# The first block product behind three norms on unscaled input, with the norm's factor applied to its result

## The reference

```python
def rms_norm(x, g):
    xf = x.astype(jnp.float32)
    y = xf * lax.rsqrt(jnp.mean(xf * xf, axis=-1, keepdims=True) + RMS_EPS)
    return (y * g.astype(jnp.float32)).astype(x.dtype)

def modulate(xn, shift, scale):
    return xn * (1.0 + scale) + shift

def sq_relu_mlp(u, w1, w2):
    a = jnp.maximum(u @ w1, 0.0)
    return (a * a) @ w2
...
    h = h + g1 * y
    h = h + g2 * sq_relu_mlp(modulate(rms_norm(h, norm2_g[l]), sh2, sc2), w_mlp1[l], w_mlp2[l])
```

## Time and profile before

| | |
|---|---|
| median of 3 runs | 2055.06 us |
| lowest and highest | 2051.90, 2056.86 us |
| the profiled execution | 2056.09 us |
| its span (first to last instruction) | 2054.2 us |
| mean granted clock of TensorE | 0.987 of full |
| PE busy | 97% |
| POOL, DVE, ACT busy | 45%, 45%, 32% |

### The profile page before, as it was taken

How to read it: one execution, slowest core, us unless ns; L and a number is a source line. 1 busy time by engine, 2 the same in 40 slices (tenths; PEclk the granted TensorE clock), 3 DMA queues, 4 the chain that set the end, 5 groups by cost and what they waited for, 6 DMA issues and landing times. The chain is left out here.

```text
span 2054.2 us, 25743 instructions
## 1 busy us (share of the span) xinstructions
PE 2002.2 (97%) x10096; PEld 1633.8 (80%) x10096; DVE 930.8 (45%) x1422; ACT 667.1 (32%) x872; POOL 920.0 (45%) x704
## 2 busy tenths in 40 slices
PE   7998899999999999999999999999999999999998
PEld 3886578888888888888888866888888878888887
DVE  0546885755748352323233265266664433223123
ACT  2322553222212332212223355356554232222122
POOL 2333345545555535445445312543444455444445
PEclk9899999999999989999999999999999999999999
DMA  8144341625334222222222202222222222222221
GB/s 350 57 143 150 131 152 75 246 91 194 147 153 175 84 83 92 102 102 83 101 102 89 82 22 78 82 83 83 72 73 82 103 82 89 96 102 100 85 82 42
DMA packets 42629, 222.92 MB, mean 109 GB/s; under 512 B 12721, under 2 KB 13233, under 8 KB 17329
## 3 DMA queue, kind: packets, MB, share of 16 engines
q1 hardware_dynamic: 42544, 221.77, 30.0%
HBM read 217.55 MB, written 2.10 MB: 107 GB/s over the span
## 5 line engine op out<-in xcount | busy, mean ns | idle before, releaser
L880 POOL TENSOR_TENSOR wl<-raw,wh 128x512 fp32r<-128x512 f32 x611 | 836.4, 1400 | 1010.9 <-ACT wh L495 911.7
L982 PE MATMUL bank<-uh,wh 128*128 128x512 f32 x1480 | 590.8, 399 | 2.2 <-DVE ul L1472 0.5
L984 PE MATMUL bank<-uh,wl 128*128 128x512 f32 x1480 | 576.9, 390 | 0.0
L983 PE MATMUL bank<-ul,wh 128*128 128x512 f32 x1480 | 576.7, 390 | 0.0
L495 ACT ACTIVATE wh<-raw 128x2048 fp32r<-128x2048 f32 (+1 forms) x149 | 281.3, 1888 | 589.6 <-PE bank L984 586.8
L982 PEld LDWEIGHTS bank<-uh,wh 128*128 128x128 f32 x1480 | 277.8, 188 | 76.8 <-issue 11.1
L984 PEld LDWEIGHTS bank<-uh,wl 128*128 128x128 f32 x1480 | 277.8, 188 | 59.2
L983 PEld LDWEIGHTS bank<-ul,wh 128*128 128x128 f32 x1480 | 278.0, 188 | 58.1 <-issue 3.6
L982 PE MATMUL bank<-ah,wh 128*128 128x512 f32 x816 | 321.3, 394 | 0.0
L984 PE MATMUL bank<-ah,wl 128*128 128x512 f32 x816 | 320.3, 393 | 0.0
L983 PE MATMUL bank<-al,wh 128*128 128x512 f32 x816 | 317.5, 389 | 0.0
(11 more groups left out here) (228 smaller groups left out, 1982.5 us busy)
## 6 DMA issues: line engine op xcount, KB each, us to landing
raw<-in_w SPq DMA_DIRECT2D x64, 1024.0 KB, 5.5
mraw<-in_w_modr SPq DMA_DIRECT2D x32, 1024.0 KB, 4.9
raw<-in_w_gu SPq DMA_DIRECT2D x22, 1024.0 KB, 4.9
raw<-in_w_hg SPq DMA_DIRECT2D x16, 1024.0 KB, 5.0
modf<-in_w_modf SPq DMA_DIRECT2D x8, 1024.0 KB, 17.9
raw<-in_w_in SPq DMA_DIRECT2D x8, 1024.0 KB, 16.7
raw<-in_w_out SPq DMA_DIRECT2D x8, 1024.0 KB, 6.0
mmid<-in_w_modr SPq DMA_DIRECT2D x8, 1024.0 KB, 4.9
```

The lines of the kernel that those rows point to most:

```text
L880: last = pool.tensor_tensor(wl[:, b % 2, k:k + 2], raw[:, b % RAW, k:k + 2], f32(wh[:, b % 2, k:k + 2]), ALU.subtract)
L982: pe.matmul(out, ah_, bh, start=first, stop=False)
L983: pe.matmul(out, ah_, bl, start=False, stop=False)
L984: return pe.matmul(out, al_, bh, start=False, stop=last)
```

## The change

At three norms, `mlp0` (block 12), `mix2` (block 80) and `ffn` (block 121), block one no longer reads the normed input. It reads high and low parts of h times the norm's gain only, `ah`/`al` (`mh`/`ml` at `mix2`). ACT writes the high part right behind each chunk's square (`plain_highs`), DVE the low part behind the addition to h (`plain_lows`). PE does the sums of the norm behind k = 1 of that block and the spread behind k = 3 (`first_product`), with no `keep_clock` there. Since the norm's factor belongs to a token, that is to a column of the result, DVE multiplies block one's result by it afterwards (`first_scale`): it copies the spread factor from its bank to `rsb` within `norm`, and behind `norm` writes bank times `rsb` into the two `tt` buffers. ACT then reads `tt` where it read the bank.

At `mlp0` the input has a shift too. Its product with block one's weights is made as a column: 16 matmuls of `raw` against the shift on PE ahead of block 11 (`shift_columns`), copied to `ccol` by DVE, and used as the bias of ACT's ReLU. Block two and all later ones read the normed input as before.

ACT splits block two no longer within `highs` but whole, between the square and plain high of chunk 6 and those of chunk 7. The set of `mod_columns` and `mod_store` that stood behind block two, four and six of mlp0's first group stands one block later. The loops of which block one was part are written out in part (mlp0's first group, mlp1's last on DVE) or in full (the FFN). The gain of `mlp0` is made before the output projection, and SP waits for block 80 and not 79 before it loads `wmask`, since `mh` and `ml` lie where it goes.

The core of the diff:

```diff
+        def plain(name):
+
+            return (mh, ml) if name == "mix2" else (ah, al)
+
+        def plain_gain(name, k):
+
+            if name == "mlp0":
+                return gm[:, 2, k:k + 1]
+            c = (V_MIX if name == "mix2" else V_FFN) + k
+            return vec[:, c:c + 1]
...
+                    if j == 4:
+                        sp.wait_ge(ccol_full, 1)
...
-                if j == 2:
-                    wait_block(sp, b0 - 1)
+                if j == 3:
+                    wait_block(sp, b0)
...
+            def plain_highs(name, ks):
+
+                for k in ks:
+                    h_wait(act, name, k)
+                    if name == "mlp0" and k == 0:
+                        act.wait_ge(gain_ready, 3)
+                    act.activation(plain(name)[0][:, k, :], h[:, k, :], ACT.Identity, scale=plain_gain(name, k)).then_inc(xhi_ready, 1)
+
+            def statistics(name, ks):
+
+                for k in ks:
+                    squares(name, h, (k,))
+                    if name in EARLY:
+                        plain_highs(name, (k,))
...
-            squares("mlp0", h, (6, 7))
+                    statistics("mlp0", (2 * (b - 9), 2 * (b - 9) + 1))
+            statistics("mlp0", (6,))
+            split(FIRST["mlp0"] + 1)
+            statistics("mlp0", (7,))
...
+                            if first and j == 0:
+                                act.wait_ge(bank_free[bi], used(b0) + 1)
+                                act.wait_ge(ccol_ready, 1)
+                                act.wait_ge(square_ready, SQ0 + 32 * layer + m - 1)
+                                act.activation(r1[:, m % 2], tt[:, half], ACT.Relu, bias=ccol[:, half:half + 1]).then_inc(first_done, 1)
+                                continue
...
+                            if j < 7 or after not in EARLY:
+                                statistics(after, (2 * (j - 4), 2 * (j - 4) + 1))
+                            else:
+                                statistics(after, (6,))
+                                split(b0 + 33)
+                                statistics(after, (7,))
...
-            highs("mlp0", lambda k: mod(0, 3, k), uh, beside=FIRST["mlp0"] + 1)
+            highs("mlp0", lambda k: mod(0, 3, k), uh)
...
+                    out, col = (aqT[:, 2 * j + half, :], V_BQ + 2 * j + half) if j < 4 else (akT[:], V_BK)
+                    if j == 0:
+                        act.wait_ge(bank_free[bi], used(b0) + 1)
+                        act.activation(out, tt[:, half], ACT.Identity, bias=vec[:, col:col + 1]).then_inc(first_done, 1)
+                        continue
...
+                    scaled = not per and n == 0
+                    act.wait_ge((bank_free if scaled else bank_full)[bi], used(b, q, per) + 1)
...
+                    act.activation(gs[:, half], tt[:, half] if scaled else bank[bi][:], ACT.Sigmoid).then_inc(gs_ready, 1)
...
+            def norm_spread(name, n=S):
+
+                i, rms = NORM[name], norm_banks(name)[1]
                 pe.wait_ge(rstd_ready, i + 1)
                 for a in range(n // P):
                     last = pe.matmul(rms[:, P * a:P * a + P], rc[:, 1, a:a + 1].to_broadcast([P, P]), ident, start=True, stop=True)
                 last.then_inc(rms_full, 1)
+
...
+            def first_product(name, b):
+
+                def ready(k):
+                    if k == 2:
+                        norm_sum(name)
+                    if k == 4:
+                        norm_spread(name)
+                    pe.wait_ge(xlo_ready, 8 * EARLY[name] + k + 1)
+
+                product(b, *plain(name), ready=ready)
 
...
+            def shift_columns(b):
+                pe.wait_ge(raw_full[b % RAW], 16 * (b // RAW + 1))
+                for half in range(2):
+                    for k in range(KC):
+                        last = pe.matmul(bank[4][:, half:half + 1], raw[:, b % RAW, k, P * half:P * half + P], mod(0, 3, k), start=(k == 0), stop=(k == KC - 1))
+                last.then_inc(ccol_full, 1)
+
             for b in range(8, 12):
+                if b == 11:
+                    shift_columns(FIRST["mlp0"])
...
+                        if first and j == 0:
+                            first_product("mlp0", b0)
+                        elif j < 4:
+                            product(b0 + j, uh, ul, q, 8, ready=normed(f"mlp{layer}") if j == (1 if first else 0) else None)
                         else:
...
+                    if k == 0 and name in EARLY:
+                        dve.tensor_copy(rsb[:], rms[:]).then_inc(rsb_ready, 1)
...
+            def plain_lows(name, ks):
+
+                hi, lo = plain(name)
+                for k in ks:
+                    dve.wait_ge(xhi_ready, 8 * EARLY[name] + k + 1)
+                    dve.scalar_tensor_tensor(lo[:, k, :], h[:, k, :], plain_gain(name, k), f32(hi[:, k, :]), ALU.mult, ALU.subtract).then_inc(xlo_ready, 1)
+
+            def first_scale(name, b):
+
+                for half in range(2):
+                    bi = bank_of(b, half)
+                    dve.wait_ge(bank_full[bi], used(b) + 1)
+                    if half == 0:
+                        dve.wait_ge(rsb_ready, EARLY[name] + 1)
+                        dve.wait_ge(ulo_ready, 8 * NORM[name] + 8)
+                    dve.tensor_tensor(tt[:, half], bank[bi][:], rsb[:], ALU.mult).then_inc(bank_free[bi], 1)
 
...
+                    dve.wait_ge(ccol_full, 1)
+                    dve.tensor_copy(ccol[:], bank[4][:, 0:2]).then_inc(ccol_ready, 1)
```

More of the change, by code:

```diff
@@ L52 @@
           "ffn": FIRST["wout2"], "final": FIRST["ffn"] + 30}
+EARLY = {"mlp0": 0, "mix2": 1, "ffn": 2}
 MOD0 = 16
@@ L673, in _ @@
             mlp(1, "mix2")
-            highs("mix2", None, uh, beside=FIRST["aq"] + 1)
+            highs("mix2", None, uh)
             act.wait_ge(lb_ready, 1)
@@ L1258, in _ @@
                 last.then_inc(yp_full, 1)
-            norm_sum("mlp1")
+            normalise("mlp1")
             mlp(1)
-            norm_sum("mix2")
             b0 = FIRST["aq"]
-            for j in range(4):
-                product(b0 + j, uh, ul, ready=normed("mix2") if j == 0 else None)
+            first_product("mix2", b0)
+            for j in range(1, 4):
+                product(b0 + j, uh, ul, ready=normed("mix2") if j == 1 else None)
             def half_and_half(b, first_by_token, q=0, per=0):
@@ L1623, in _, with group @@
                     mod_store(MOD_MID // 2 + (b - 8) // 2)
+            plain_lows("mlp0", (6, 7))
             dve.wait_ge(mcol_used, MOD0 // 2)
-            gain_of(2, modc[:, 32:40], vec[:, V_G2:V_G2 + 8])
             def mlp(layer):
                 b0, n0 = FIRST[f"mlp{layer}"], 32 * layer
-                with dve.Fori(0, 4) as q:
+                def group(q, last=False, first=False):
                     for j in range(8):
+                        if first and j == 0:
+                            first_scale("mlp0", b0)
                         if layer == 0 and j < 6:
@@ L1636, in mlp @@
                                 add_to_h(b0 + j, m, mod(layer, 5, m), q, 8)
+                                if last and j > 4:
+                                    plain_lows("mix2", (m - 2,))
                                 continue
@@ L1639, in mlp @@
                             dve.wait_ge(bank_free[bi], used(b0 + j, q, 8) + 1)
+                            if first and j == 0:
+                                dve.wait_ge(first_done, 2 * EARLY["mlp0"] + half + 1)
                             dve.wait_ge(a_lo, SQ0 + n0 + m - 1 + 8 * q)
@@ L1906, in _ @@
             dve.memset(stat[:, 4, 1:2], 0.0).then_inc(zv_ready, SQ0)
-            with dve.Fori(0, 2) as q:
+            first_scale("ffn", b0)
+            for q in range(2):
                 for j in range(0, 8, 2):
-                    hidden(j, j, j, q, 12)
+                    hidden(12 * q + j, 8 * q + j, j)
                 for j in range(8, 12):
                     for half in range(2):
-                        add_to_h(b0 + j, 2 * (j - 8) + half, None, q, 12)
+                        add_to_h(b0 + 12 * q + j, 2 * (j - 8) + half, None)
             for j in range(0, 6, 2):
```

110 lines of the change are left out of this document (69 added, 41 removed).

## The result

The changed kernel takes 2066.64 us (median of 5 runs, 2064.91 to 2070.26), the kernel before 2055.06 in the same session (5 runs, 2051.90 to 2056.86): a ratio of 1.0061, 95% interval 1.0050 to 1.0072. It is slower, by 11.6 us; 2067.0 was forecast. In a second session the changed kernel took 2067.86 beside 2055.71. The profiled execution of after was the slowest of its five (2070.26, span 2068.4), so the traces lie 14.2 us apart and the medians 11.6.

What follows compares the result with a forecast made beforehand. PE, busy 97% of the span, was taken as the bound. Later third blocks 1.6, shift's product 3.9 and clock loss 6.6 made 12.1 us, so about 2067 against 2055.06; range 2058 to 2073.

Steps and rivals of the forecast that it cites:

- Block one starts at T, PE is through with block two at T+25.2: At each norm, T being when PE ends the block before: PE runs blocks one and two without waiting until T+25.2.
- DVE's norm starts at T+8.7: At each norm, DVE's norm starts once the spread has landed, 8.7 us after PE ends the block before; previously T+4.8.
- The third block at T+31.6, 31.2 and 30.2: Block three's start at mlp0, mix2 and ffn, set by its weights, counted from PE's end of the block before.
- in all 1.6 us: Block three's lateness against before, like for like: 0.8 at mlp0, 0.5 at mix2, 0.3 at ffn.
- Stalls of 6.4, 6.0 and 5.0: PE stands still between blocks two and three at mlp0, mix2 and ffn for these times in us.
- The shift's product, 3.9: Ahead of block 11, 32 one-column records take 3.9 us of PE's time; bounds 3.6 and 7.3.
- Rival 3: Narrow products also lower the clock: 1.9 us more on the shift's product, 1.7 for what follows; 2070.8 us, chance 0.12.
- The clock behind the stalls, 6.6: Half clock after each of PE's three stalls costs 2.2 us, the mean of two earlier stalls; ends 0 and 8.3.
- Rival 1: The same chain at the three norms, but the clock holds: 2060.6 us, chance 0.18.
- The sum: Whole kernel: late third blocks, shift's product and clock loss add 12.1 us, giving about 2067 us.
- Rival 2: Block three's weights are ready at T+25.2 at each norm: 15.8 us gained, less 3.9; 2043 us, chance 0.10.

Runs made afterwards that it cites:

- experiment 8: The changed kernel with the product that spreads the sums issued one pair of passes earlier in block one, at all three norms: 2063.10 us, ratio 1.0037.
- experiment 3: The changed kernel with 20 keep-clock products on PE ahead of block three at each of the three norms: 2061.36 us, ratio 1.0037.
- experiment 7: The changed kernel with the early block at mix2 and ffn only, block three's weights split early there, no shift product: 2042.85 us, ratio 0.9944.
- experiment 6: The changed kernel with block three's weights split early, block four's transfer ahead of the modulation loads, shift product in one piece: 2048.93 us, ratio 0.9970.
- experiment 10: experiment 7 with the shift's product added ahead of block eleven, its result read by nothing: 2049.73 us, ratio 0.9970.
- experiment 9: experiment 7 without its early split: block three's weights split where the changed kernel splits them: 2059.20 us, ratio 1.0020.

## Why the prediction was right, step by step

**Block one starts at T, PE is through with block two at T+25.2.** Shown: block one starts without a wait at all three norms, and at mlp0 PE stands still from 367.12 - 6.51 = 360.61 = T+24.9.

**DVE's norm starts at T+8.7.** It started at T+8.5, and experiment 8 shows that a microsecond there is about a microsecond of stall at each norm.

**The third block at T+31.6, 31.2 and 30.2.** It came at T+31.4, at mix2 at 1137.25 - 1107.28 = T+30.0, at ffn at 1714.63 - 1684.27 = T+30.4. The copy to `rsb` took 0.68, the 0.69 that was chosen. The term "in all 1.6 us" was mis-sized: like for like the blocks were 0.6 later, 0.7 earlier and 0.5 later (T+30.8, 30.7 and 29.9 before), 0.4 in all. At mix2 1.2 us too much had been charged, in many small steps and not in one. Of it 0.8 stood already where DVE's scaling begins, at T+21.0 and not T+21.8:

```profile
1115.68 0.75 DVE L1560 SCALAR_TENSOR_TENSOR tt<-h,vec,bank 128x512 f32<-128x512 f32 x1 [2.99 <-PE bank L1108]
...
1128.32 1.29 DVE L1593 TENSOR_TENSOR tt<-bank,rsb 128x512 f32<-128x512 f32 x2
```

**Stalls of 6.4, 6.0 and 5.0.** Measured 6.5, 5.2 and 5.5, 17.2 in all against 17.4.

**The shift's product, 3.9.** 3.93 in the first trace, 3.49 where the clock held to its end (315.20 to 318.69), 3.9 on average, so the choice stands. What the forecast put at nothing is the half clock behind it, 2.9 in that trace and 2.0 on average. Rival 3, which I had given 0.12, had the cause: narrow products bring the clock down. It put 1.9 on the product itself, where the first trace has 0.4 (3.93 less 3.49), and 1.7 on what follows, where it has 2.9. Its other part, that the sums in block one bring the clock down too, did not come: 1.00 from 335 to 342 us.

**The clock behind the stalls, 6.6.** 2.2 + 2.8 + 2.5 = 7.5 in the first trace, 5.0 in the second, 6.6 on average over the four with these stalls. The mean of the two stalls of before was right, with a spread from trace to trace that the forecast did not name. Rival 1, the clock holds, is refuted; experiment 3 shows by what it would have been true, work on PE in the stall, and what it is worth (5.3 us measured).

**The sum.** Forecast 1.6 + 3.9 + 6.6 = 12.1. By the first trace 0.4 + 3.9 + 2.9 + 7.5 = 14.7, against 9.7 + 2.0 + 3.0 = 14.7 by the offsets of the same instruction (the traces differ by 14.2, since stretches that the change does not touch add 0.8, -1.1 and -0.2). That trace is of the slowest execution, and both clock terms are high in it. With the averages the sum is 0.4 + 3.9 + 2.0 + 6.6 = 12.9, against medians that differ by 11.6 and 12.2; the interval of the first ratio, 10.3 to 14.8 us, holds all of these. That 12.1 met the medians so closely is in part luck, two errors against each other: chains charged 1.2 too much, the clock behind the shift not at all.

**Rival 2, the weights come in time.** Not so in this kernel, and its condition, 5 to 6 us less between the spread and POOL's end, was the right one: experiment 7 meets it by moving `wh` ahead of the scaling (POOL ends at 1111.63 + 6.02 = T+23.8 at mix2, before T+25.2), and gains 12.2 us by the medians, 10.3 by the traces at the two norms. At mlp0 it is not enough. Experiment 6 and experiment 10 differ by the early block at mlp0 alone (and the load order it needs): 2048.93 and 2049.73, 6.2 and 6.0 below the kernel before in their sessions, no measurable difference. There the early block returns nothing. In experiment 6 it pays 1.63 and 1.05 us of wait in the group behind the norm, and 1.6 us of clock (0.74 over the six microseconds from 371.5), about 4.2 of the 5.6 that rival 2 gave this norm; the shift's product is paid on top.

## What to carry to other kernels

Work put into a wait moves whatever the wait was for to a later time: follow the chain behind it (here spread, norm, scaling, activation, next weights) to the first block that reads from it, and put the preparation of that block ahead of the chain in each engine's order. With the same early block, that order alone decided between 3.5 us lost and 12 us gained (experiments 9 and 7). The stalls of 5.2 to 6.5 us on TensorE were paid once as a wait, and by 1.4 to 3.0 us more each as half clock behind it, not the same in every trace.

## What the runs showed of the hardware that was not expected

One-column products in a row lowered the clock without any gap on PE. 32 records in 3.5 to 4.7 us, and the granted clock fell to 0.50 within them or right behind them for some 3 to 7 us, in six of seven traces of kernels that run them in one piece; with full passes between them it stayed at 1.00 (both traces). The sums, 16 narrow records between full passes, left it at 1.00 too. The Trainium skill's page "TensorE: Matmul & The Clock Gate", section "Why this matters for your kernels", speaks of idle gaps between bursts; here PE had none, so by that rule nothing would be lost, and the measured loss is up to 2.9 us.

A one-column product between full passes takes 0.24 us of PE's time, as much as in a row (3.9 over 16): spreading it hides nothing.
